# Layer 0 of a hybrid decoder trunk: where the gate block's products stand in the HGRN scan, which engine splits eight weight pieces, and where the head-norm weights are applied

## What is computed

```python
g_qkv, g_z, g_b, g_a, h_q, h_f, h_i, h_g = split_cols(h @ w_in, EVEN_SPLITS)
...
o_a = rms_norm(o_a, gdn_norm_w) * jax.nn.silu(split_heads(g_z, GDN_HEADS))
...
def hgrn2_recurrence(q, k, i, log_f):     # per chunk of 64 tokens, 4 heads, dk = dv = 128
    def step(state, inp):
        q_i, k_i, i_i, b_i = inp
        dmat = jnp.exp(jnp.where(causal, b_i[:, :, :, None, :] - b_i[:, :, None, :, :], -jnp.inf))
        attn = jnp.einsum('bhtk,bhsk,bhtsk->bhts', q_i, k_i, dmat)
        o = (jnp.einsum('bhtk,bhkv->bhtv', q_i * jnp.exp(b_i), state)
             + jnp.einsum('bhts,bhsv->bhtv', attn, i_i))
        b_last = b_i[:, :, -1:, :]
        state = (state * jnp.exp(b_last[:, :, 0, :])[..., None]
                 + jnp.einsum('bhsk,bhsv->bhkv', k_i * jnp.exp(b_last - b_i), i_i))
        return state, o
...
o_b = rms_norm(o_b, hgrn_norm_w) * jax.nn.silu(split_heads(h_g, HGRN_HEADS))
return jnp.concatenate([merge_heads(o_a), merge_heads(o_b)], axis=-1) @ w_out
```

## Time and profile before

| | us |
|---|---|
| median of three (lowest, highest) | 1273.44 (1273.24, 1281.03) |
| the profiled execution, and its span | 1275.61, 1273.5 |
| TensorE busy | 1137.3 (89%) |
| VectorE, ScalarE, GpSimd busy | 663.3, 592.0, 416.0 |
| the eight HGRN scan steps up to the first row block | 319.7 to 347.9 in the span |

### The profile page before, as it was taken

The page is one execution under the profiler, slowest core; times in us unless marked ns, Lnnn a source line. Parts: engine busy times, 40 slices in busy tenths (PEclk is TensorE's granted clock), DMA queues, the critical chain, the costliest instruction groups (busy, mean ns, idle before and its releaser), DMA issues.

```text
span 1273.5 us, 19313 instructions
## 1 busy us (share of the span) xinstructions
PE 1137.3 (89%) x6971; PEld 914.7 (72%) x6971; DVE 663.3 (52%) x908; ACT 592.0 (46%) x843; POOL 416.0 (33%) x350
## 2 busy tenths in 40 slices
PE   6998999999997499995699999999989993999990
PEld 5786888788786388784588668886668883788770
DVE  4334334388635599994606122430221335899984
ACT  5555243232424288985233332233322242789871
POOL 4332212110132233445254225442233251334432
PEclk9989999999798699998699999999989995999995
DMA  8331311112036669995443223332122166599955
GB/s 250 69 81 34 68 36 49 37 37 99 17 92 240 208 230 367 368 371 184 178 124 93 66 74 98 86 106 62 62 83 83 50 224 241 165 363 360 373 188 207
DMA packets 89282, 194.86 MB, mean 153 GB/s; under 512 B 19901, under 2 KB 21241, under 8 KB 88186
## 3 DMA queue, kind: packets, MB, share of 16 engines
q1 hardware_dynamic: 67562, 160.00, 38.1%
q10 hardware_dynamic: 11856, 17.07, 3.8%
q0 software_dynamic: 9792, 16.80, 3.6%
HBM read 189.63 MB, written 23.07 MB: 167 GB/s over the span
## 4 chain that ended last, share of the span: by engine, by line
PE 79%; DVE 9%; ACT 5%; DMA 3%; issue 2%; POOL 1%; POOLq 0%; DVEq 0%; SPq 0%; ACTq 0%
PE ps L583 22%; PE ps L585 20%; PE ps L584 20%; PE ps L2211 3%; PE ps L2220 2%; PE ps L2021 2%; ACT wh L1143 1%; DMA hs<-arena 1%; PE ps L1877 1%; DMA arena<-hs,slot_rows 1%; DVE arena L1327 1%; DMA arena<-y 1%; PE ps L2194 1%; PE ps L1908 1%; PE ps L2203 1%
## 5 line engine op out<-in xcount | busy, mean ns | idle before, releaser
L743 POOL TENSOR_TENSOR wl<-raw,wh 128x1024 fp32r<-128x1024 f32 x100 | 241.5, 2423 | 487.7 <-ACT wh L909 487.4
L583 PE MATMUL ps<-wh,hT_hi 128*128 128x512 f32 x928 | 379.8, 409 | 17.9 <-DVE hT_lo L1375 8.1
L585 PE MATMUL ps<-wh,hT_lo 128*128 128x512 f32 x928 | 367.2, 396 | 0.0
L584 PE MATMUL ps<-wl,hT_hi 128*128 128x512 f32 x928 | 366.5, 395 | 0.0
L909 ACT ACTIVATE wh<-raw 128x1024 fp32r<-128x1024 f32 x116 | 122.0, 1059 | 251.4 <-PE ps L585 230.3
L583 PEld LDWEIGHTS ps<-wh,hT_hi 128*128 128x128 f32 x928 | 177.7, 191 | 62.9 <-issue 15.1
L585 PEld LDWEIGHTS ps<-wh,hT_lo 128*128 128x128 f32 x928 | 177.2, 191 | 39.1
L584 PEld LDWEIGHTS ps<-wl,hT_hi 128*128 128x128 f32 x928 | 177.9, 192 | 35.0 <-issue 1.0
L583 PE MATMUL ps<-hT_hi,wh 128*128 128x512 f32 x288 | 118.2, 410 | 7.3 <-ACT arena L1052 5.3
L1698 DVE TENSOR_TENSOR wl<-arena,wh 128x1024 fp32r<-128x1024 f32 x96 | 117.6, 1225 | 12.7 <-ACT wh L1143 4.7
L1698 DVE TENSOR_TENSOR wl<-raw,wh 128x1024 fp32r<-128x1024 f32 x92 | 112.2, 1225 | 18.0 <-ACT wh L909 9.8
(11 more groups left out here) (291 smaller groups left out, 1318.5 us busy)
## 6 DMA issues: line engine op xcount, KB each, us to landing
raw<-in_moe_w_gate_up_dram SPq DMA_DIRECT2D x64, 512.0 KB, 8.7
arena<-in_moe_w_gate_up_dram SPq DMA_DIRECT2D x64, 512.0 KB, 8.5
raw<-in_odd_w_in_dram SPq DMA_DIRECT2D x48, 512.0 KB, 3.7
raw<-in_even_w_in_dram SPq DMA_DIRECT2D x32, 512.0 KB, 4.6
arena<-in_moe_w_down_dram SPq DMA_DIRECT2D x32, 512.0 KB, 7.9
raw<-in_moe_w_down_dram SPq DMA_DIRECT2D x32, 512.0 KB, 9.6
arena<-y ACTq DMA_DIRECT2D x8, 1024.0 KB, 8.2
raw<-in_odd_w_out_dram SPq DMA_DIRECT2D x16, 512.0 KB, 3.5
```

The costliest lines, as they stand in the source:

```text
L583: nc.tensor.matmul(dst, lh, rh, start=first, stop=False)
L584: nc.tensor.matmul(dst, lh, rl, start=False, stop=False)
L585: return nc.tensor.matmul(dst, ll, rh, start=False, stop=last)
L743: pool.tensor_tensor(wl[:, i % NSPL, :, :], raw_at(i), wh[:, i % NSPL, :, :].bitcast(F32), ALU.subtract).then_inc(lo_pool, 1)
```

## The change

Five things, all in layer 0.

1. `lo` of pieces 26 to 33 goes from VectorE to GpSimd.
2. Block 7 is moved: its piece 0 to between level 4 and level 5, the other three to between the steps of the scan, as halves (tokens or output tiles 0, 1 and 2, 3). No dense product is left between levels 3 and 4, between level 5 and `hstate`, or ahead of the scan.
3. The state products of chunks c and c+1 are issued together in an even `hscan`, head by head with the two halves of the rows in turn; VectorE's state addition now also waits for the chunk's output product.
4. The sums of squares come from ScalarE's accumulator, one activation per head (128 columns) in place of one for four heads (512); VectorE's reduction goes.
5. The norm weights are one value per partition, applied where the transposed tiles are read from PSUM (`yT`: ScalarE's scale, VectorE's multiply-and-subtract); two loads that broadcast them, and VectorE's multiplication in `evac_gate`, go.

```diff
-DVE_LO = range(26, 34)
 def lo_by_dve(i):
-    return i in DVE_LO or any(m + 2 <= i < m + 6 * NE for m in MOE_PIECE)
+    return any(m + 2 <= i < m + 6 * NE for m in MOE_PIECE)
...
-        if n > 2:
-            s.append(("piece", 7, n - 3))
-    s += [("hstate",), ("piece", 7, 3)]
-    for T in range(NT + 1):
-        if T < NT:
-            s.append(("hscan", 2 * T))
+        if n == 4:
+            s.append(("piece", 7, 0))
+    s.append(("hstate",))
+    dense = [part(7, kp, *ts) for kp in (1, 2, 3) for ts in ((0, 1), (2, 3))]
+    for T in range(NT):
+        s.append(("hscan", 2 * T))
         if T > 0:
             s.append(("onorm", 1, (T - 1,)))
-        if T < NT:
-            s.append(("hscan", 2 * T + 1))
+        s += dense[2 * T:2 * T + 1 + T // 2] if T < 3 else []
+        if T == 2:
+            s.append(("evac_gate", 7, 0))
+        s.append(("hscan", 2 * T + 1))
         if T > 0:
-            s += [("oscale", 1, (T - 1,)), ("evac_gate", 7, T - 1)]
-        if T > 1:
-            s.append(("yT", 0, 0, (T - 2,)))
-        if T > 2:
-            s.append(("rows", 8, T - 3))
-    s += [("yT", 0, 0, (NT - 1,)), ("rows", 8, 2), ("rows", 8, 3), ("evac", 8)]
+            s.append(("oscale", 1, (T - 1,)))
+        s += dense[2 * T + 1:2 * T + 2] if T < 2 else [("evac_gate", 7, T - 1), ("yT", 0, 0, (T - 2,))]
+    s += [("onorm", 1, (3,)), ("rows", 8, 0), ("oscale", 1, (3,)), ("evac_gate", 7, 3)]
+    s += [("yT", 0, 0, (2,)), ("rows", 8, 1), ("yT", 0, 0, (3,)), ("rows", 8, 2), ("rows", 8, 3), ("evac", 8)]
...
+                        scale = head_w[:, g:g + 1] if l == 0 else 1.0
+                        A(act.activation(HTH[:, 4 * g:4 * g + 4, cols(T)], v3(tile(name), 4), ACT.Copy, scale=scale), s_("hT_hi_made"))
...
-                    A(act.activation(onsq[:, T % 2, :], Y0[:, T, 512 * w:512 * w + 512], ACT.Square), s_("o_sq"))
+                    for h in range(NH):
+                        A(act.activation(onsq, Y0[:, T, 512 * w + P * h:512 * w + P * h + P], ACT.Square,
+                                         accum_out=oss[:, 4 * T + h:4 * T + h + 1]), s_("o_sq"))
...
+                        D.read(stt(lo, v3(tile(nm), 4), head_w[:, g:g + 1], hi.bitcast(F32), ALU.mult, ALU.subtract), nm)
...
                 tile_is_ready(dve, ("hs", c))
+                tile_is_ready(dve, ("ho", c))
...
-                        D(tt(v3(z, 4), v3(z, 4), bc_m(wgt[:, :]), ALU.mult))
...
-                t = open_tile(("hs", c))
-                for h in range(NH):
-                    ins = mm(t[:, cols(h)], KDT[r, T, cols(h)], HI[r, T, cols(h)], start=True, stop=True)
-                done(ins)
+                if c % 2 == 0:
+                    t = [open_tile(("hs", c + n)) for n in range(2)]
+                    for h in range(NH):
+                        for n in range(2):
+                            ins = mm(t[n][:, cols(h)], KDT[half(n), T, cols(h)], HI[half(n), T, cols(h)], start=True, stop=True)
+                            if h == NH - 1:
+                                done(ins)
```

More of the change, by code:

```diff
@@ L265, in side_tiles @@
     if k == "hscan":
-        return [(("ho", step[1]), "act"), (("hs", step[1]), "dve")]
+        c = step[1]
+        return [(("ho", c), "act")] + [(("hs", c + n), "dve") for n in range(2 if c % 2 == 0 else 0)]
     if k == "score":
@@ L319, in build @@
         vnew = sb("vnew", [P, 512])
-        gnw = sb("gdn_w", [P, P])
-        hnw = sb("hgrn_w", [P, P])
+        head_w = sb("head_w", [P, 2])
         ar = sb("arena", [P, 22528])
@@ L386, in build @@
         KDT = v3(reg(8192, 2048), 4)
-        onsq = v3(reg(7168, 1024), 2)
+        onsq = reg(7168, P)
         raw_vec = reg(21000, 128)
@@ L692, in _ @@
                   (dtb, a["gdn_dt_bias"].broadcast_to([P, 4])), (alog, a["gdn_a_log"].broadcast_to([P, 4])),
-                  (gnw[:, :], a["gdn_norm_w"].broadcast_to([P, P])), (hnw[:, :], a["hgrn_norm_w"].broadcast_to([P, P])),
+                  (head_w[:, 0:1], a["gdn_norm_w"].rearrange("a p -> p a")), (head_w[:, 1:2], a["hgrn_norm_w"].rearrange("a p -> p a")),
                   (wba_raw, a["even_w_in"][0].rearrange("(p k) c -> p k c", k=KD)[:, :, 2048:2056])]
-            for dst, src in small_ones:
-                sp.dma_start(dst, src).then_inc(s_("consts_loaded"), 16)
+            with nc.allow_non_contiguous_dma(reason="one value of a head's norm weight per partition"):
+                for dst, src in small_ones:
+                    sp.dma_start(dst, src).then_inc(s_("consts_loaded"), 16)
             def moe_loads(l):
@@ L977, in yT @@
                         tile_is_ready(act, name)
-                        A(act.activation(HTH[:, 4 * g:4 * g + 4, cols(T)], v3(tile(name), 4), ACT.Copy), s_("hT_hi_made"))
+                        scale = head_w[:, g:g + 1] if l == 0 else 1.0
+                        A(act.activation(HTH[:, 4 * g:4 * g + 4, cols(T)], v3(tile(name), 4), ACT.Copy, scale=scale), s_("hT_hi_made"))
             def gates_act():
@@ L1374, in lo_tiles @@
                     dve.wait_ge(s_("hT_hi_made"), hT_hi_count(nm))
-                    D.read(tt(HTL[:, 4 * g:4 * g + 4, cols(T)], v3(tile(nm), 4), HTH[:, 4 * g:4 * g + 4, cols(T)].bitcast(F32),
-                              ALU.subtract), nm)
+                    hi, lo = (x[:, 4 * g:4 * g + 4, cols(T)] for x in (HTH, HTL))
+                    if name[0:2] == ("yT", 0):
+                        D.read(stt(lo, v3(tile(nm), 4), head_w[:, g:g + 1], hi.bitcast(F32), ALU.mult, ALU.subtract), nm)
+                    else:
+                        D.read(tt(lo, v3(tile(nm), 4), hi.bitcast(F32), ALU.subtract), nm)
             def gate_inputs():
@@ L1483, in onorm @@
             def onorm(w, Ts):
-                for T in Ts:
-                    dve.wait_ge(s_("o_sq"), 4 * w + T + 1)
-                    D(dve.tensor_reduce(oss[:, 4 * T:4 * T + 4], v3(onsq[:, T % 2, :], 4), AX.X, ALU.add), s_("sq_reduced"))
+                dve.wait_ge(s_("o_sq"), NH * (4 * w + Ts[-1] + 1))
                 a_, b_ = 4 * Ts[0], 4 * Ts[-1] + 4
@@ L1572, in evac @@
                 elif which in ("z", "hg"):
-                    wgt = gnw if which == "z" else hnw
                     w = int(which == "hg")
@@ L1792, in _ @@
                     hgrn(step)
[L1793 to L1796, removed]
                 elif k == "hscan":
```

7 lines of the change are left out of this document (removed).

## The result

| | before | after |
|---|---|---|
| median of 20 runs (lowest, highest), us | 1274.01 (1269.92, 1281.03) | 1278.15 (1276.11, 1284.1) |
| profiled execution, and its span | 1275.61, 1273.5 | 1278.23, 1276.3 |
| level 2 to the second block's transposes | 73.67 | 78.76 |

A forecast was written before the change was run, and what follows sets the result against it. TensorE, busy 89% of the span, bounds the kernel, with VectorE nearly full at the levels. Scan −10.4, levels +8.7 and first row block +3.4 sum to +1.7 us: median from 1273.44 to 1275, range 1265 to 1281.

The forecast's parts named there:

- Sign and class: Whole kernel: slower by +1.7 us, which counts as no change, within 1% (chance 0.91).
- the high rivals: Clock falls in the levels, 1279 (chance 0.17); paired state products do not overlap, 1279 (0.05); they reach 1281.
- Scan, −10.4: Scan to first row block: paired state products and moved pieces gain 10.4 us, if the clock stays at 2.4 GHz.
- Levels, +8.7: Level 2 to scan: TensorE's waits for VectorE, 9.55 us together where before had 0.85, lose 8.7 us.
- a rival with 0.17: Between pieces 27 and 28 the clock falls, slower than before: +3 to +6 us, 1279; chance 0.17.
- That a split on GpSimd holds VectorE for its whole length: Levels: a GpSimd split costs VectorE up to 2.4 us, where VectorE's own split cost 1.22.
- the first rival: Levels: splits on GpSimd do not hold VectorE; 5.8 us less, 1269, or 1265 without piece 35's wait; chance 0.28.
- First row block, +3.4: First row block: TensorE waits 4.05 us for piece 35's late split; block takes 9.65 us in place of 6.26.
- Norm weights 0: Norm weights, reductions, loads: no separate gain, as removed multiplications are already in VectorE's times; loads between −0.5 and +0.5 us.
- "From 354.17 on everything is shifted alike": After the first row block's end, all later work keeps its order and shifts by the same sum, +1.7 us.

The follow-up runs named there:

- Experiment 1: The changed kernel with the first row block put ahead of the fourth sum of squares again; ratio 1.0007 to the kernel before.
- experiment 5: The kernel before with only the norm weights applied at the transposed tiles, squares and VectorE's reduction kept; ratio 0.994.
- 4: The kernel before with both norm parts alone: sums of squares from ScalarE's accumulator and weights at the transposes; ratio 0.9931.
- 12: The changed kernel with splits back on VectorE, first row block ahead of the fourth sum, piece 28 in halves around level 4; ratio 0.9957 to before.
- experiment 9: The kernel before with only block 7 moved as in the change, in halves, and the last `onorm` ahead of `rows(8, 0)`; ratio 1.0082.
- 7: The kernel before with both norm parts and the paired state products, nothing moved, splits on VectorE; ratio 0.9943.
- 8: The kernel before with norm parts and pairs, plus piece 31 in quarters behind chunks 0 to 3 of the scan; ratio 0.9932.
- experiment 6: The kernel before with the paired state products alone; ratio 0.996.

## Why the prediction came out as it did

**Sign and class** were right, and the time lies in the range of 1265 to 1281; the size, +1.7 us, fell short of 4.1 (2.5 to 5.7). The median, 1278.15, is just above the forecast's own range of 1272 to 1278 (chance 0.50), on the side of the high rivals. By its own steps:

- **Scan, −10.4: right** (−10.3). Its inside differed a little. A pair takes 1.16 us and the next row starts 1.09 later, less than the 1.25 taken; the wait ahead of the last pair was 1.03 in place of 1.3, and one of 0.40 came behind it. Against that, the halves of pieces take 2.95 us each and not 2.8, and the transposes 0.3 more than laid out. That the sum came out to 0.1 us is in part luck. The clock stayed at 1.00 (335 to 341), as the forecast said it must. By the rows of before at 1.2 GHz (336.19 to 347.91) about 5 of the 10 us are this clock.
- **Levels, +8.7: the term that was mis-sized** (+11.2). TensorE's waits came close to those laid out: 0.63, 0.79, 2.90, 1.85, 1.14 and 0.84, 8.15 us, where seven waits and 9.55 had been summed. What was left out of the sum is the clock: 0.8 twice at level 4 and 1.8 on piece 28, 3.4 in all. Of this 0.8 is hidden, since the second wait at level 4 was 1.85 in place of 2.65; the 2.6 left are about the 2.5 us by which the term was short. I had it as a rival with 0.17, at the right place and with +3 to +6 as its price for the whole, and the measured +4.1 lies in that range. So of the forecast and its rivals it is this one that came true, with the waits of the forecast in it. The trace of before had a stretch at 0.50 behind small products, and I put more weight on the 15 us that it took there than on TensorE having been nearly busy in them, which it is not between bare levels. What decides when the clock falls stays open (below).
- **That a split on GpSimd holds VectorE for its whole length: right.** The trace of after shows it and experiments 2 and 3 show it from both sides: splits back on VectorE in after, 3.6 us less in the stretch; splits alone on GpSimd in before, 1.0027. This decides against the first rival (0.28), and for the rule on shared interfaces that the Trainium skill gives in the GPSIMD Engine Reference, section 8, over what its section 4.1 taken alone would make of it; the price is measured only here.
- **First row block, +3.4: right in mechanism, 0.8 short.** The wait was 3.40 where 4.05 stood. In ScalarE's timeline four squares take 1.74 us together, not 1.9, and in GpSimd's the root takes 1.01, not 1.51. But the clock fell during the wait, and the block's last matmuls and the transposes behind ran at 1.2 GHz. Experiment 1 shows the order of `onorm` and `rows` to be 3.1 us of the block; the wait of 1.5 us that is left is for what else stands ahead of `hi(35)` on ScalarE, a gate and the copies of `yT`, which I had counted among ScalarE's work but not as a wait of its own.
- **Norm weights 0: right for what I asked, and the wrong question.** In after their gain is within the scan and level terms. Taken alone they are the largest gain of the change in the stretch (−5.2 us); by the times (ratio 0.994) they can't be told from the pairs (0.996). In experiment 5 the scan is 4 us shorter than before (24.2 against 28.2). The waits in it are 0.7 us more, so the gain there is the clock, up to 339.8 where before it fell by 336. Why 0.7 us less VectorE work at each gate should hold the clock up is not shown, and experiment 3 had most of that gain with the gates of before.
- **"From 354.17 on everything is shifted alike": only roughly.** By the starts of ScalarE's high parts in the two traces, after lies 5.8 us behind at 368 to 386, 4.1 in the first MoE, 3.1 and then 2.5 in layer 1, 2.2 in the second MoE and 2.8 at the end. The 1.4 us of the second row block had been left out, and some 3 us come back later. Part of this belongs to the trace of before: between 386 and 442, where after gains 1.7 us on it, the traces of experiments 2, 3, 4, 5 and 12 gain 0.6 to 2.1 us as well. The experiments' ratios differ from their stretches by −3.7 to +2.2 us. The rest is open; it is of the size by which the kernel before varies from run to run.

**Where the gain went.** Singly the parts give, in the stretch, +1.4 (splits, counted from level 1), −5.8 (norm), −3.2 (pairs) and +8.2 (move), +0.6 in all; together they give +5.1. Two reasons offer themselves. Norm and pairs shorten the same scan, the norm by the clock and the pairs mostly so: −7.1 together, not −9.0, and in the times −7.3 where singly −8.8 and −5.1 stand, which is clear of the intervals. With the move alone (experiment 9) the clock stayed up until 349 in a scan that ended at 353.7, so that in after little of this is left for them to give. And move and splits both fall on levels that no dense work covers any more; this second reason is argued, since the move and the splits were not run together without the other parts. In the times the four add to about 0 us, give or take 6 (an estimate from their intervals), so that there the difference to 4.1 is not clear of noise. The measured order of versions agrees: nothing moved, splits on VectorE, norm part with or without pairs or quarters stand at 0.9931 to 0.9943, within each other's intervals; the best that keeps the move is 0.9957 (0.9941 to 0.9973), whose interval overlaps theirs. The version to keep is experiment 4, as the simplest with the lowest ratio; I can't tell it from 5, 7 or 8, and not surely from 12.

**Open.** What makes the clock fall in one scan and not in another. From 338 to 344 it was 0.50 before, 0.51 in experiment 6, 0.72 in 3 and 5, 0.83 in 7 and 1.00 in 4, and the busy time of TensorE in the 6 us ahead (4.70, 2.92, 4.43, 4.70, 4.24, 4.97) does not put them in that order. At the levels it fell behind every wait of over 2 us (2.51 to 5.34), but twice behind one of 1.1 as well (experiments 1 and 12), which after had without a fall. No run varied a wait alone. Nor was `hi(35)` tried ahead of the copies of `yT`, which should take out most of the last 1.5 us of the row block, since the two copies take 1.4 (an estimate).

## What to carry over

Dense work between short dependent steps is a cover for another engine's chain: before it is moved to where it also helps, lay out that chain without it, and count its longest TensorE waits with the slow clock behind them: here each of 2.5 us or more cost 1.6 to 3.4 us beyond itself (1.6 in experiment 3, 3.4 in after). An idle GpSimd is not free when VectorE's operations have both inputs in SBUF: a job on it costs VectorE up to the job's whole length, so it belongs where VectorE reads PSUM or has nothing to do. And a change of several parts hides its best one: the plainest part here, a multiplication folded into a read that happens anyway, makes the kernel faster alone (0.994), while the whole makes it slower. Before such a gain is put down to the work that went away, compare the waits and the clock: here the waits grew, and the clock gave more than all of the gain in the scan.

## What the runs showed of the hardware

- A VectorE operation with two SBUF inputs that runs into a GpSimd split ends some 0.5 us after it (1.3 to 2.8 us in place of 0.69), one of 1.13 us alone 0.9 us after it (3.14); one that reads PSUM is untouched (0.43 and 0.74, a state addition 0.69). GpSimd is held too: 2.64 in place of 2.35.
- State products of 64 rows, four of one half and four of the other in turn, take 1.16 us, exactly as long as four of one half alone.
- Behind waits of 2.5 to 2.9 us between products of 1.1 us the clock of TensorE was at 1.2 GHz for up to 10 us (in after 0.53 and 0.50 from 293 to 303), in which the next dense piece took 7.1 to 8.0 us in place of 5.6. Behind waits of 1.1 us it fell in two traces and not in others.
- The same scan, in the same order, took 28.2 us in one trace and 24.8 in another, with the clock down for a longer and a shorter time.
- A square of 128 columns with accumulator takes 0.31 and its read 0.19 us, and four of them follow each other every 0.44, 1.74 in all; a copy with a scale from SBUF takes 0.71 in place of 0.60.
